# TensorE's loop over expert blocks in a mixer-and-MoE layer: four blocks a turn, each body under its own comparison

## What is computed

```python
def _moe(h, router_w, router_b, w_gu, b_gu, w_down, b_down):   # h: (1024, 1024)
    logits = (h @ router_w + router_b)                          # 32 experts
    top_v, top_i = lax.top_k(logits, TOP_K)                     # 4 a token
    gates = jax.nn.softmax(top_v, axis=-1)
    ...                                                         # rows sorted into blocks of one expert each
    def expert_block(args):
        xblk, e = args
        gu = xblk @ w_gu[e] + b_gu[e]                           # (rows, 1024) @ (1024, 2048)
        gate = jnp.minimum(gu[:, ::2], 7.0)
        up = jnp.clip(gu[:, 1::2], -7.0, 7.0)
        act = (up + 1.0) * gate * jax.nn.sigmoid(1.702 * gate)
        return act @ w_down[e] + b_down[e]                      # (rows, 1024) @ (1024, 1024)
    yb = lax.map(expert_block, (xb, block_e))
    return sum of y * gate over each token's four rows
```

## Time and profile before

| | |
|---|---|
| runs timed | 3, median 3001.78 us (3001.09 to 3004.14) |
| profiled execution, its own time | 2975.63 us |
| span of its instructions | 2973.8 us |
| TensorE matmul busy | 2605.9 us (88%) |
| weight loads busy | 2261.4 us (76%) |
| VectorE, ScalarE, GpSimd busy | 1820.0 (61%), 1545.4 (52%), 744.9 us (25%) |
| mean granted TensorE clock | 0.955 |
| DMA | 536.87 MB, mean 181 GB/s |

### The profile page before, as it was taken

How to read it: one execution, slowest core, us unless ns; L and a number is a source line. 1 busy time by engine, 2 the same in 40 slices (tenths; PEclk the granted TensorE clock), 3 DMA queues, 4 the chain that set the end, 5 groups by cost and what they waited for, 6 DMA issues and landing times. The chain is left out here.

```text
span 2973.8 us, 133311 instructions
## 1 busy us (share of the span) xinstructions
PE 2605.9 (88%) x55861; PEld 2261.4 (76%) x55861; DVE 1820.0 (61%) x2086; ACT 1545.4 (52%) x1832; POOL 744.9 (25%) x594
## 2 busy tenths in 40 slices
PE   8999997988989895799978999798999998889972
PEld 2444556888878553799978999788999998789962
DVE  2344984444454587657787717878174567873884
ACT  3522543433333545556686627767263566763773
POOL 1211004535454013122222312122122222212212
PEclk9999997999999995999999999999999999999996
DMA  9400001000000326867898818989264569884875
GB/s 368 172 29 31 1 1 40 25 14 18 25 18 11 117 105 218 318 224 266 275 367 281 288 28 295 326 287 351 49 238 154 197 232 325 282 331 135 309 283 188
DMA packets 124468, 536.87 MB, mean 181 GB/s; under 512 B 12524, under 2 KB 13536, under 8 KB 91600
## 3 DMA queue, kind: packets, MB, share of 16 engines
q1 hardware_dynamic: 107104, 481.80, 43.9%
q0 software_dynamic: 14464, 47.79, 7.2%
q10 hardware_dynamic: 2832, 6.37, 0.6%
HBM read 496.99 MB, written 38.92 MB: 180 GB/s over the span
## 5 line engine op out<-in xcount | busy, mean ns | idle before, releaser
L2160 PE MATMUL ps<-qkv,weights 128*128 128x64 f16 x10496 | 960.4, 195 | 138.9 <-DVE qkv L1707 57.1
L2160 PEld LDWEIGHTS ps<-qkv,weights 128*128 128x128 f16 x10496 | 934.1, 99 | 154.0 <-issue 85.4
L2161 PE MATMUL ps<-qkv,weights 128*128 128x64 f16 x10496 | 959.8, 195 | 4.1 <-issue 4.1
L2162 PE MATMUL ps<-qkv,weights 128*128 128x64 f16 x10496 | 959.6, 195 | 1.6 <-issue 1.6
L2162 PEld LDWEIGHTS ps<-qkv,weights 128*128 128x128 f16 x10496 | 934.8, 99 | 4.4 <-issue 4.4
L2161 PEld LDWEIGHTS ps<-qkv,weights 128*128 128x128 f16 x10496 | 934.7, 99 | 2.7 <-issue 2.7
L1668 DVE SCALAR_TENSOR_TENSOR weights<-hT,weights 128x2048 f16<-128x2048 f32 x256 | 594.3, 2374 | 197.8 <-ACT weights L1147 189.1
L1147 ACT ACTIVATE weights<-hT 128x2048 f16<-128x2048 f32 x256 | 520.5, 2092 | 101.5 <-DMA hT<-in_w_gu_dram 93.0
L2177 PE MATMUL ps<-qkv,weights 128*128 128x64 f16 x5248 | 473.2, 193 | 17.9 <-DVE weights L1673 15.4
L2177 PEld LDWEIGHTS ps<-qkv,weights 128*128 128x128 f16 x5248 | 462.2, 98 | 21.1 <-DVE weights L1673 18.7
L2179 PE MATMUL ps<-qkv,weights 128*128 128x64 f16 x5248 | 472.9, 193 | 2.3 <-issue 2.3
(11 more groups left out here) (385 smaller groups left out, 4121.5 us busy)
## 6 DMA issues: line engine op xcount, KB each, us to landing
hT<-in_w_gu_dram SPq DMA_DIRECT2D x256, 1024.0 KB, 7.9
qkv<-in_w_down_dram SPq DMA_DIRECT2D x128, 1024.0 KB, 5.4
weights<-in_w_ada_dram SPq DMA_DIRECT2D x12, 2048.0 KB, 17.2
qkv<-in_w_in_dram SPq DMA_DIRECT2D x4, 2048.0 KB, 7.8
hT<-decay_rows SPq DMA_DIRECT2D x20, 256.0 KB, 3.4
hT<-beta_rows SPq DMA_DIRECT2D x20, 256.0 KB, 4.1
qkv<-in_x_dram ACTq DMA_DIRECT2D x8, 512.0 KB, 6.5
weights<-in_w_in_dram SPq DMA_DIRECT2D x2, 2048.0 KB, 14.7
```

Source lines behind the costliest of these rows:

```text
L2160: pe.matmul(dst, ghi[k][:, b, c], xT[:, 0, k, :], start=first, stop=False, skip_group_check=True)
L2161: pe.matmul(dst, ghi[k][:, b, c], xT[:, 1, k, :], start=False, stop=False, skip_group_check=True)
L2162: last = pe.matmul(dst, glo[k][:, b, c], xT[:, 0, k, :], start=False, stop=end, skip_group_check=True)
```

## The change

TensorE's loop makes a quarter as many turns, rounded up (24 in place of 94). A turn holds the body of the old loop four times, for blocks 4u + 1 to 4u + 4, each copy under its own comparison with `nprev`. What a body does, its order, its waits and counts are the same, and the other engines' programs are as they were.

```diff
 GS = 5
+RUN = 4
 SLOT = KD * 512
...
             turn_x(2)
             down(0)
-            with pe.Fori(1, MAXB) as t:
-                with pe.If(t <= nprev):
-                    for k in range(GK):
-                        gate_up(t + 1, k)
-                    turn_x(t + 2)
-                    turn_y(t - 1)
-                    down(t)
+            with pe.Fori(0, (MAXB - 1 + RUN - 1) // RUN) as u:
+                for i in range(RUN):
+                    t = u * RUN + (i + 1)
+                    with pe.If(t <= nprev):
+                        for k in range(GK):
+                            gate_up(t + 1, k)
+                        turn_x(t + 2)
+                        turn_y(t - 1)
+                        down(t)
             turn_y(nprev)
             down(nlast)
             turn_y(nlast)
```

## The result

The changed kernel takes 3409.73 us (median of 4 runs, 3397.85 to 3435.19) against 3001.94 us: the ratio is 1.1387, 95% interval 1.1346 to 1.1428. It is slower by 408 us. The forecast said 3570 us, 3300 to 3850. The profiled execution took 3416.41 us, 440.8 us more than the profiled one of before (2975.63); this is the difference that the traces can explain.

The account below looks back on a forecast made before the run. It took TensorE to bound two loop turns in three, weight loading and conversion the rest. -22 + 420 + 90 + 80 = +568 us on the 3001.8 us median gave 3570 us, range 3300 to 3850.

Parts of the forecast that it names:

- (a): Instruction stream in the loop is hidden and only jumps cost: +148 us, 3150 us; chance 0.10.
- (b): TensorE's instruction store holds all four bodies, so the kernel is faster: about -10 to -25, 2985 us; chance 0.06.
- (c): Stream stalls charged in full, each piece meeting a loaded DMA, jumps at upper ends: +868, 3870 us; chance 0.12.
- Step 1: Block boundaries in TensorE's loop: three in four lose the branch back, 60 x 0.36 us: -22 us.
- Step 2: Inside the loop's bodies: 376 pieces of instructions fetched again, slow under loaded DMA: +420 us, between 271 and 663.
- The lower end's two assumptions: In the loop, weight bytes fix the loaded time, and long turns absorb stalls up to 29.4 us each: +271 us together.
- Step 3: Loop's branch back, once in four blocks, to a piece no longer held: 19 returns x 4.7 us, +90 us.
- Step 4: After the last real block: 20 jumps over passed bodies and back, 4.5 us each, unhidden: +80 us.

Follow-up runs that it names:

- RUN = 1: The changed kernel with one body a turn, the block's number still formed from the turn's: ratio 0.9998 to the kernel before.
- RUN = 2: The changed kernel with two bodies a turn in place of four: 3423.81 us, ratio 1.1444 to the kernel before.
- the small loads: Loop's weight loads cut to 128 columns of each row, in the kernel before and the changed one: 2934.95 and 3095.34 us.

## Why the prediction was right, and where its sizes were off

**The cause** stood in the rows of before, and the runs bear it out: the body was held, four bodies aren't (RUN = 1 against RUN = 2, 150 matmuls of padding against 290), and a piece fetched in sequence costs TensorE much time only beside loaded DMA engines (the small loads: some 25 us in place of 292). Rivals (a) and (b) fail on the 292 us of the stream, (c) on its size.

**Step 1** (boundaries), -22 us: measured -20.

**Step 2** (stream), +420 between 271 and 663: measured 292. This is the term that was mis-sized, and it is most of the error. The lower end's two assumptions were nearly true, and I chose 149 us above them. The loaded time is nearly fixed: 0.62 x 2022.6 = 1254 us now, 1205 before. And the long turns absorbed nearly all they could: the wait for VectorE's low halves went from 63.0 to 11.1 us. My reason for the higher value, that late conversions keep TensorE waiting, didn't hold.

The granted clock has a part in this, though a small one. In the loop it fell from 0.98 to 0.92. In the timeline some 4390 of the weight loads of the products start 40 to 100 ns after the one before, where 830 did in the kernel before; the usual distance is 29 ns, and at the lower of the clock's two levels (1.2 instead of 2.4 GHz) it is 50 to 55. Their excess over 29.3 ns is 107 us against 20. But most of these 87 us aren't a cost of their own. More than half of the excess lies between packets at a DMA share above 0.8, and there the median spacing is 6.29 us where the clock was below 0.85 (39 of them) and 6.24 at full clock (102): a slow piece just waits less for the next one, as in the earlier trace rows. At lower shares the slow ones do take longer (4.8 us for 3.8 below a share of 0.2). Summed over all spacings against the mean at full clock and the same share, my estimate is some 20 us of the 292.

**Step 3** (returns), +90: measured +77; 81.2 / 19 = 4.3 us each, where I had 5.5 before taking off what queued matmuls cover.

**Step 4** (end), +80: measured +91. The size is near, the reason was not. My 4.5 us a jump assumed loaded engines at first and less later. The opening return took 4.9 us and the first jump 8.0, beside the reload of x1 (DMA share 0.9 to 1.0). All the others took 4.5 to 5.1 us, with the DMA share at 0.04 to 0.07, while returns in the loop begin at 3.3 beside idle engines. The records of the instruction queue show the difference. In such a return of the loop one packet starts 1.0 us into the branch and takes 0.9 to 1.4 us. At the end two packets run side by side in each of these branches, the first from about 0.5 us, the second from about 1.0, and they take 1.0 to 2.4 us each: 40 packets for 20 jumps. By its place the first is the piece behind the one just entered, which nobody will use, and the second is the target. That the two slow each other down is the likely reason for the missing microsecond; no run separated it.

**The sum.** Against the traces' 441 us I had 568. The rest of the distance between 3570 and 3409.73 is the reference: I added the forecast to the median of before, 26 us above its profiled execution, while the profiled execution of the changed kernel lay 7 us above its own median. One slip in the range: its upper sum has +80 for the end, where the term's own upper end was +115, so it should have been 3870 and not 3835. The result is far from either.

## What to carry to other kernels

On TensorE, a loop that is held in the instruction store costs a fraction of a microsecond a turn, and one that is larger is fetched anew in every turn, whole. Before unrolling, count the instructions of the turn (a matmul is two) in pieces of 256, and add one for the place where the loop begins: here seven pieces stayed and eight did not. Then look whether the DMA view of the loop lists an instruction queue. The fetch of the next piece in sequence hides where DMA engines are idle, and stands in line where the kernel streams weights. Bodies that are passed over by a comparison aren't free either, once their code isn't held: they cost 91 us here. Where the count is known at run time, let it end the loop.

## What the runs showed that I had not expected

Jumping over code that isn't held costs 4.5 to 5.1 us even at a DMA share of 0.04 to 0.07, but the distance alone doesn't decide it: with RUN = 2 the same jumps fell to 0.2 us within the second turn. While TensorE was starved between pieces its granted clock was lower too (0.92 over the loop for 0.98), yet beside loaded DMA engines a piece took no longer for it. And in the kernel before, a gap of 10 us at the end was hiding a collision of the last scatters with the reload of x1: with 8 us of the gap taken away, the scatters took nearly all of it back.
